# Two transformer blocks on one core: the normed context in tiles of its own, at other addresses, and a pair of mLSTM products six steps later

## The reference, cut to what matters

```python
def modulate_2(a, g, shift, scale):
    return rms_norm_2(a, g) * (1 + scale) + shift
...
def project(h):                       # mLSTM: h is the modulated latents, or the modulated context
    q, k, v, o, z, g = jnp.split(h @ w_in, ML_SPLITS, axis=-1)
...
hn = _merge_heads(_head_rms(h_sum, head_g)).astype(o.dtype)
return (jax.nn.sigmoid(o) * hn * jax.nn.silu(z)) @ w_out
```

## Time and profile before

| | |
|---|---|
| median of 3 runs | 2565.44 us (2563.82 to 2571.71) |
| the profiled execution's own time | 2564.46 us |
| its span, first to last instruction | 2562.7 us |
| TensorE, busy share of the span | 98% |
| VectorE / ScalarE / GpSimd, busy share | 51% / 32% / 9% |
| mean granted TensorE clock | 0.995 of full speed |

### The profile page before, as it was taken

One profiled execution on the slowest core, in us unless ns is written; L12 is line 12 of the kernel. 1 busy time (PEld: TensorE's weight loads), 2 busy tenths in 40 slices (PEclk: granted clock), 3 DMA queues, 4 the chain that ended last, 5 costly groups with the idle time before them and its releaser, 6 DMA issues.

```text
span 2562.7 us, 31059 instructions
## 1 busy us (share of the span) xinstructions
PE 2515.1 (98%) x13030; PEld 2022.1 (79%) x13030; DVE 1304.6 (51%) x2065; ACT 825.6 (32%) x1172; POOL 229.9 (9%) x186
## 2 busy tenths in 40 slices
PE   7999999999999999999999999999999999999999
PEld 4888888898767879888888786887787788687766
DVE  6665443436346766767747333422432332576663
ACT  3211111124234354232224323122222312245663
POOL 0100000012110002000000110110210101210001
PEclk9999999999999999999999999999999999999999
DMA  7344333311202112555532110210110021011001
GB/s 294 116 136 162 137 135 119 128 66 66 73 27 75 41 50 97 191 176 175 177 107 75 50 50 17 77 56 25 58 66 34 17 83 66 17 67 67 34 34 50
DMA packets 45115, 223.55 MB, mean 87 GB/s; under 512 B 4737, under 2 KB 6961, under 8 KB 30129
## 3 DMA queue, kind: packets, MB, share of 16 engines
q1 hardware_dynamic: 43008, 215.24, 23.7%
q10 hardware_dynamic: 1968, 6.34, 0.7%
HBM read 219.46 MB, written 2.10 MB: 86 GB/s over the span
## 4 chain that ended last, share of the span: by engine, by line
PE 91%; DVE 5%; ACT 2%; issue 1%; POOL 0%; DMA 0%; SPq 0%; DVEq 0%; ACTq 0%; POOLq 0%
PE ps L442 40%; PE ps L455 12%; PE ps L1560 8%; PE ps L422 3%; PE ps L3621 3%; PE ps L3168 3%; PE ps L1261 2%; PE ps L2957 2%; PE ps L880 1%; PE ps L3738 1%; PE ps L3837 1%; PE ps L3861 1%; DVE wl L393 1%; PE ps L2547 1%; PE ps L2083 1%
## 5 line engine op out<-in xcount | busy, mean ns | idle before, releaser
L393 DVE TENSOR_TENSOR wl<-stage,wh 128x2048 fp32r<-128x2048 f32 (+2 forms) x155 | 326.6, 2107 | 511.3 <-ACT wh L385 511.1
L442 PE MATMUL ps<-hh,wh 128*128 128x512 f32 x1120 | 445.2, 398 | 1.2 <-DVE m_X L2981 1.2
L442 PE MATMUL ps<-hl,wh 128*128 128x512 f32 x1120 | 437.4, 391 | 0.0
L442 PE MATMUL ps<-hh,wl 128*128 128x512 f32 x1120 | 436.7, 390 | 0.0
L385 ACT ACTIVATE wh<-stage 128x2048 fp32r<-128x2048 f32 (+2 forms) x155 | 267.0, 1722 | 454.5 <-PE ps L455 251.5
L442 PEld LDWEIGHTS ps<-hh,wh 128*128 128x128 f32 x1120 | 211.1, 189 | 48.2 <-issue 6.7
L442 PEld LDWEIGHTS ps<-hh,wl 128*128 128x128 f32 x1120 | 210.8, 188 | 44.8
L442 PEld LDWEIGHTS ps<-hl,wh 128*128 128x128 f32 x1120 | 211.2, 189 | 42.5 <-issue 1.2
L654 DVE CUSTOM_DVE_ANT_0 left<-direct,cond_rows,vecs 128x1024 bf16<-128x1024 f32 x168 | 207.0, 1280 | 0.0
L455 PE MATMUL ps<-hl,wh 128*128 128x256 f32 x688 | 194.7, 283 | 0.0
L455 PE MATMUL ps<-hh,wl 128*128 128x256 f32 x688 | 194.7, 283 | 0.0
(11 more groups left out here) (608 smaller groups left out, 4656.5 us busy)
## 6 DMA issues: line engine op xcount, KB each, us to landing
stage<-wts SPq DMA_DIRECT2D x110, 1024.0 KB, 4.8
direct<-wts SPq DMA_DIRECT2D x104, 512.0 KB, 4.3
stage<-wts SPq DMA_DIRECT2D x24, 768.0 KB, 4.3
stage<-wts SPq DMA_DIRECT2D x22, 512.0 KB, 3.3
group<-wts SPq DMA_DIRECT2D x6, 512.0 KB, 6.2
first<-wts SPq DMA_DIRECT2D x6, 512.0 KB, 9.7
x<-xin SPq DMA_DIRECT2D x4, 512.0 KB, 7.3
group<-wts SPq DMA_DIRECT2D x2, 1024.0 KB, 9.5
```

Source lines behind the costliest of these rows:

```text
L393: dve.tensor_tensor(l[:, 0:w], stage[m % 2][:, 0:w], h[:, 0:w].bitcast(F32), SUB).then_inc(*w_low.up(m))
L442: i = pe.matmul(bank[b[f]][:, :], w[:, k, cols], s[:, k, LAT], start=k == 0 and a == 0, stop=k == nk - 1 and a == 2, skip_group_check=True)
```

## The change

The normed values get tiles by side: latents `hhl`, `hll` of `[128, 8, 512]` and context `hhc`, `hlc` of `[128, 8, 256]`. `Parted` hands a slice to the one or the other, so that the code which uses `hh` and `hl` is unchanged. The context tiles begin 192 bytes past a multiple of 512 from where `hh` began, the latents' at a multiple. To make room, small tiles move: `G`, `cb` and `a_rq` go into gaps, and `DIRECT`, with all that lies there (`m_yl` too), moves by 320 bytes. `HREG` and the area behind it move by 512. In the mLSTM the two spreads leave the middle of the Q projection and stand behind its step n = 12 (half 1, k = 5), for heads 1 to 3.

```diff
+class Parted:
+    def __init__(self, context, latents):
+        self.context, self.latents = context, latents
+    def __getitem__(self, i):
+        p, k, s = i
+        if s.stop <= C:
+            return self.context[p, k, s]
+        return self.latents[p, k, slice(s.start - C, s.stop - C)]
...
-    DIRECT = o
-    direct = [at(f"direct{i}", [128, 1024], F32, o + 4096 * i) for i in range(3)]
-    o += 12288
+    DIRECT = o + 320
+    direct = [at(f"direct{i}", [128, 1024], F32, DIRECT + 4096 * i) for i in range(3)]
+    o += 12800
     HREG = o
-    hh = at("hh", [128, 8, T], F32R, o)
-    hl = at("hl", [128, 8, T], F32R, o + 24576)
-    o += 49152
+    hh = Parted(at("hhc", [128, 8, C], F32R, o + 32960), at("hhl", [128, 8, L], F32R, o))
+    hl = Parted(at("hlc", [128, 8, C], F32R, o + 41152), at("hll", [128, 8, L], F32R, o + 16384))
+    o += 49664
...
-    G = at("G", [128, 5, 8, 2], F32, o + 128)
-    H = at("H", [128, 2, 8, 2], F32, o + 128 + 320)
+    G = at("G", [128, 5, 8, 2], F32, DIRECT - 320)
+    H = at("H", [128, 2, 8, 2], F32, o + 128)
...
-    cb = at("cb", [128, 8, 6], F32, o)
-    o += 192 + (-(base + o + 192)) % 64
+    cb = at("cb", [128, 8, 6], F32, DIRECT + 12288)
+    o += (-(base + o)) % 64
...
+    def output_beside(pe, h, n):
+        if n == 12:
+            normed_output_pe(pe, h)
...
                 by_features(pe, ml(c0 + 256 * h), SETS[j], hh, hl, True, not fresh, (lambda c, k: pe.wait_ge(*h_low.at(4, c, k))) if fresh else None,
-                            (lambda: normed_output_pe(pe, h - 1)) if h and j else None,
-                            (lambda n: sums_beside(pe, h - 1, n)) if h and j == 0 else None)
+                            None, (lambda n: (output_beside if j else sums_beside)(pe, h - 1, n)) if h else None)
```

More of the change, by code:

```diff
@@ L290, in build @@
     cs2 = at("cs2", [128, 8, 2], F32, o + 64)
-    G = at("G", [128, 5, 8, 2], F32, o + 128)
-    H = at("H", [128, 2, 8, 2], F32, o + 128 + 320)
-    lgd = at("lgd", [128, 8], F32, o + 576)
-    lgt = at("lgt", [128, 16], F32, o + 608)
-    o += 704
+    G = at("G", [128, 5, 8, 2], F32, DIRECT - 320)
+    H = at("H", [128, 2, 8, 2], F32, o + 128)
+    lgd = at("lgd", [128, 8], F32, o + 256)
+    lgt = at("lgt", [128, 16], F32, o + 288)
+    o += 384
     MVA = o
     o += 4096
-    cb = at("cb", [128, 8, 6], F32, o)
-    o += 192 + (-(base + o + 192)) % 64
+    cb = at("cb", [128, 8, 6], F32, DIRECT + 12288)
+    o += (-(base + o)) % 64
     AREA = o
@@ L351, in build @@
     group_in = [[signal(f"group_in{i}_{j}", 16) for j in range(4 if i == 0 else 2)] for i in range(len(GROUPS))]
-    rows_at = [DIRECT, DIRECT + 4096, DIRECT + 8192, AREA + 40960, AREA + 45056, HREG + 18432]
+    rows_at = [DIRECT, DIRECT + 4096, DIRECT + 8192, AREA + 40960, AREA + 45056, HREG + 12288]
     rows_chunk = [at(f"first{i}", [128, 1024], F32, o_) for i, o_ in enumerate(rows_at)]
@@ L662, in build @@
     factor1 = area("factor1", [128, T], F32, 67584)
-    row1 = [at(f"row1_{i}", [128, 512], F32, HREG + 43008 + 2048 * i) for i in range(2)]
+    row1 = [at(f"row1_{i}", [128, 512], F32, HREG + 28672 + 2048 * i) for i in range(2)]
     M1first = M1[:, 0:16, :].rearrange("p (a k) s -> p a k s", a=2)
@@ L3506, in build @@
     sms = [area(f"a_sm{i}", [128, 6, 4], F32, o + 28672 + 96 * i) for i in range(4)]
-    rqs = [area(f"a_rq{j}", [128, 16], F32, o + 29056 + 64 * j) for j in range(4)]
+    rqs = [at(f"a_rq{j}", [128, 16], F32, HREG + 49344 + 64 * j) for j in range(4)]
     araw = [at(f"a_raw{i}", [128, L], F32, DIRECT + 2048 * i) for i in range(2)]
```

## The result

The changed kernel took **2549.43 us** (median of 4 runs, 2548.05 to 2551.94) against 2565.54 us for the kernel before (2563.82 to 2571.71). The ratio is 0.9934, 95% interval 0.9916 to 0.9952: 16.1 us less, and not the 26.7 that the sum gave. The profiled execution took 2549.97 us, and its span is 2548.2.

The account below looks back on a forecast made before the run. PE, with 91% of the span on the chain of waits, was taken to bound the kernel. Addresses -15.0 and spreads -11.7 summed to -26.7 us, giving 2538.7 us, with a range of 2534 to 2548.

Parts of the forecast that it names:

- The context on L455, -12.9 us: Context products of L455: 43 chunks, each going from 5.75 to 5.45 us at distance 192, -12.9 us.
- `m_yl`, -1.6: 288 context products with `m_yl` on L455, moved to distance 320, go from 118.8 to 113.1 ns: -1.6 us.
- `third`, +0.1: Context of the `third` chunk, 48 products going to distance 384, which no row has: +0.1 us.
- context products of other lines: 240 context products outside L455 (first chunks, after norms, attention keys): between 0 and -1.5, taken as -0.7 us.
- 256 weight columns over context: Context held stationary with 256 weight columns moving, 144 products: between 0 and -1.0, taken as -0.5 us.
- L1560, +0.6: Context held stationary with 512 weight columns moving, 288 products from distance 0 to 320: +0.6 us.
- the -15.0 of the prediction: All address terms together, the context on L455 the largest: -15.0 us.
- The spreads, -11.7: PE's wait for DVE's diagonals before the spreads in three heads, and the clock loss behind it, vanish: -11.7 us.
- rival 3: The spreads' wait only shrinks, half of the 11.7 us kept: 2544.6 us; chance 0.09.
- rival 2: Context reaches only 118.0 ns, as the hidden layer in the other product order: 2550.4 us; chance 0.07.
- Rival 1: The addresses make no difference and only the spreads' wait goes: 2553.7 us; chance 0.05.
- Rival 4: Latents become slower, 233.4 instead of 226.9 ns over 4656 products, +30.3 us: 2584.0 us; chance 0.03.

Follow-up runs that it names:

- Runs 9: Changed kernel with each normed chunk entering its context stream in another way, in turn (twelve entries); only rates were read, no time given.
- 11: Changed kernel with the last latents product cut into two of 256 columns in every chunk with a context: 2549.26 us, ratio 0.9934.
- Run 1: Changed kernel with the spreads back in their old place, so only the addresses differ from the kernel before: 2561.56 us, ratio 0.9977.
- run 8: Changed kernel with the context's three products of a k reordered: high by high, low by high, high by low: 2553.1 us, ratio 0.9936.
- 12: Kernel before, context at distance 0, with the last latents product cut into two of 256 columns in every chunk with a context: 2570.21 us, ratio 1.0006.

## Why the prediction was wrong

- **The context on L455, -12.9 us: this step failed.** The prediction put it as 43 chunks by 5.75 - 5.45 us, with the 113.5 ns of `third` as the rate of distance 192. It measured 5.65 us in 40 chunks and about 5.47 in three: 40 x 0.10 + 3 x 0.28 = 4.8 us. The row was read rightly; the step that failed is carrying its rate to another neighbourhood. `third`'s stream stands behind latents at distance 192, at 233.4 ns each, and a normal chunk's stream stands behind latents at distance 0. Runs 9 and 11 give the normal chunk the 113.8 ns once its entry is another. What exactly in an entry does it is not settled: for the normed context a fp32 product, a repeat or a cut of 64 + 192 doesn't, cuts of 128 + 128 and of the latents' last product do. What in the engine carries it over, no run shows.
- **The hidden layer was not in the sum at all**, since its distance stays 320. It went from 113.1 to 117.8 ns: 9 chunks x 36 x 4.7 = +1.5 us. The prediction used it as the witness for 113 and didn't ask what held it there.
- **`m_yl`, -1.6.** Head 1's four chunks reached 113.3 ns, the eight of heads 2 and 3 117.9, against 118.8: 96 x 5.5 + 192 x 0.9 = 0.7 us.
- **`third`, +0.1.** 5.70 us instead of 5.45, +0.25. Its distance became 384, a multiple of 128, and 118.7 ns came of it.
- **The other terms.** Added up product by product over the two traces, outside waits and falls of the clock: context products of other lines -0.3 us (the sum had -0.7), 256 weight columns over context -0.3 (it had -0.5), the mLSTM output's latents -0.7 where the sum took 0. A product of these takes (1627.21 - 1621.66)/24 = 231 ns before and (1623.47 - 1617.98)/24 = 229 after.
- **L1560, +0.6.** Right: the tiles at distance 320 mostly rotate through 232, 226 and 229 ns, 229 in the mean.
- **Not foreseen, to the good:** products of 512 columns off distance 0 have two rates as well. The hidden layer's first latents went from 233.3 to 229.2 ns: 36 take 155.59 - 147.34 = 8.25 us by the fence below, 156.52 - 148.12 = 8.40 before. The 96 products of the retention output `r_yh`, `r_yl` did the same. Three chunks of 36 products and these 96, by 4.2 ns, are 0.9 us.

```profile
147.34 0.40 PE L435 MATMUL ps<-uh,wh 128*128 128x512 f32 x1
...
155.59 0.28 PE L447 MATMUL ps<-uh,wh 128*128 128x256 f32 x1
```

- The addresses together: -4.8 + 1.5 - 0.7 + 0.25 + 0.6 - 0.3 - 0.3 - 0.7 - 0.9 = -5.4 us. The normed latents, at 226.7 ns instead of 227.3 in many chunks, give 0.3 more. Run 1 measured -4.2 with an interval of -2.3 to -9.7, which holds this and not the -15.0 of the prediction.
- **The spreads, -11.7: right**, in place, mechanism and size. DVE's diagonals are ready at 1579.95 in head 1 and PE arrives at 1581.36, the pair takes 1.29 us, no new wait shows at L2970 or in the output projection, and rival 3 did not come. The changed kernel less run 1 is 2549.4 - 2561.6 = -12.1 us, of medians from two chips. One reading was off without harm: the prediction says of head 2 that the clock came back earlier there, but in that trace it did not fall at all (granted 1.00 from 1794 to 1802; 0.54 from 2015 to 2017 in head 3).
- **The rivals.** The time landed on rival 2's 2550.4 us, to which 0.07 was given. It was right in its rate, 118, and wrong in its reason: not the order of the products (run 8) but what ran ahead. That its time came out is in part luck, since it left out the hidden layer's loss and the latents' gain. Rival 1 is refuted by runs 11 and 12: with the same cut, moving one operand of the same products gives 113.8 or 120.0 ns. The Trainium skill, "TensorE: Matmul & The Clock Gate", Part 2, in the step on LDWEIGHTS, says that loading the next tile's weights doesn't steal read bandwidth from the running matmul. As a rule by which the distance could not matter it fails for these fp32r streams; whether read bandwidth is what a stream at distance 0 lacks, no run shows. Rival 4 is refuted: the latents stay at 227 ns.

The forecast held 0.76 because `third` and the hidden layer agreed. They were two rows of one condition, and the row that disagreed, 118.0 at the same distance as 113.1, was put down to its order without a second row for it.

## What to carry to other kernels

A rate read in one stream belongs to that stream's neighbourhood: before it is carried to another, ask what runs directly ahead of it in both, and price the other observed rate at the same distance as a likely case, not a stray one. In a stream of products like these, 256 fp32r columns wide, keep the moving operand's address off the stationary one's modulo 128 bytes, then look whether the quick rate is taken; a free cut of one product at the border of two streams may turn it. And compare runs at an equal mean clock when a gain is a few microseconds. One caution goes with that: a change that removes falls of the clock, as the moved spreads do in heads 1 and 3, has part of its gain from the clock itself, and such a comparison hides that part.

## What the runs showed that was not expected

- Streams of 256 fp32r columns have three levels here: 118.6 to 120.0 ns at distances 0, 128, 256 and 384; 117.8 or 113.3 to 114.0 at 192 and 320; 117.8 at 64, where the quick rate was never seen. The two lower levels belong to one distance: a stream keeps its rate for its 36 or 48 products, and what ran before decides which it is (the hidden layer's nine chunks at 113.3 behind context at 0, 64, 128 and 256, at 117.8 behind whole context chunks at 192).
- Streams of 512 columns are quickest at distance 0, 226.7 to 227.3 ns; off it they take 229 in the mean or 233.
- A cut at a border of streams toggles: cutting every hidden-layer chunk put one in three at 113.3 and the others at 117.8, leaving them whole, behind a cut first chunk of their stage, put all nine at 113.3.
- The time of a run follows its mean granted clock: the kernel before took 2577.3 to 2577.7 us at 0.990, about 2571 at 0.992, 2565.5 at 0.995 and 2561.9 at 0.997. That is about 2 to 3 us for 0.001, more than most terms of this sum.
